# One stage of 160 units by token halves from the output projection to the store

## The chip, the cores and the metric

The kernel runs on one core of a Trainium2 chip. The time is that of the device in microseconds, the lower the better. The core's engines run their own queues and meet at semaphores: TensorE (PE) multiplies into PSUM, VectorE (DVE), ScalarE (ACT) and GpSimd (POOL) work on tiles in SBUF, VectorE and ScalarE also on PSUM, and SyncE (SP) issues the transfers.

## The reference

One residual block on 1024 tokens of width 1024. The part that matters begins when the two mixers, an RWKV-7 group and a sparse attention group, have written their rows:

```python
        mix = jnp.concatenate([y_rwkv, y_dsa], axis=-1).astype(x.dtype) @ w_out[i]
        x = x + rms_norm(mix, norm_mix_post[i])
        h = rms_norm(x, norm_ffn_pre[i])
        f = jnp.square(jax.nn.relu(h @ w_ffn1[i])) @ w_ffn2[i]
        x = x + rms_norm(f, norm_ffn_post[i])
        gate = jax.nn.sigmoid(rms_norm(x, norm_ple_pre[i]) @ w_ple_gate[i])
        x = x + rms_norm((p[i] @ w_ple[i]) * gate, norm_ple_post[i])
```

`rms_norm` divides each token by the root of the mean of its squares over the 1024 features and multiplies by a gain. The feed-forward width is 4096, p has 256 features.

## The kernel before

Everything lies feature-major: a tile is 128 features by tokens, eight such blocks are a full activation. Each fp32 operand of a large product is split into a rounded part (`hi`) and a remainder (`lo`), and a product is three matmuls, hi by hi, hi by lo and lo by hi. A weight tile is 128 x 1024 (512 KB): ScalarE rounds it (`Weights.round`, line 436), GpSimd subtracts (`Weights.remainder`, line 440), SyncE loads the next one into one of two slots when the remainder is made (line 431).

The stages run one behind the other, each in a block of its own with a barrier at its end. `project_out` multiplies the rows by 8 tiles of `w_out`, for both halves of 512 tokens per tile, and has the squares of its result added on GpSimd (line 215). `norms` then does the norm of the result, adds it to x and does the norm that the next product needs. For a half it takes the squares on ScalarE (line 203), sums them over the partitions with small matmuls on TensorE (lines 221 and 228), takes the root on ScalarE (line 234), inverts it and builds a diagonal on VectorE (lines 238 and 241), spreads it by a matmul (line 246), scales by it on VectorE (line 253), adds to x on VectorE and GpSimd in turn (lines 348 and 383), rounds on ScalarE (line 324) and takes the remainder on VectorE and GpSimd in turn (lines 353 and 390). `ffn` is a loop of 8 chunks of 4 up units (1024 features in, 128 out) and 4 down units (512 in, 256 out), each for all 1024 tokens, 48 matmuls. VectorE takes relu, square, rounding and remainder of an up unit (lines 573 to 577) and adds a down unit to the total (line 581). A second `norms` follows, then `per_layer`, 8 units of gate product, sigmoid on ScalarE (line 700), product with p (lines 737 to 739) and their product on VectorE (line 752), then `norms` once more and `store_x`, one transfer of 4 MB (line 1997).

The order on every engine is the order in which the code is written. The stages before the output projection are not touched.

## Time and profile before

| | us |
|---|---|
| median of 3 runs | 2121.1 (2120.21 to 2123.97) |
| the profiled execution | 2117.07 |
| its span, first to last instruction | 2115.2 |
| mean granted TensorE clock | 0.916 |
| output projection, first to last product | 1015.0 to 1110.5 |
| norms | 1110.5 to 1180.5 |
| feed-forward | 1180.5 to 1878.5 |
| norms | 1878.5 to 1959.0 |
| gate stage | 1959.0 to 2070.8 |
| last norm and store | 2070.8 to 2115.2 |

Positions are microseconds from the span's start. Busy time is that of instructions; waiting, branching and issuing transfers are not counted. Matmuls are pipelined: one is shown as some 390 ns long, though the next one starts sooner, so the distance of their starts is what a product costs. A granted clock of 1.0 is 2.4 GHz, 0.5 is 1.2 GHz. "out<-in" names the tile that is written and the tiles that are read, without their numbers.

### The profile page before, as it was taken

How to read it: one execution, taken by the hardware profiler on the slowest of the kernel's cores; microseconds unless marked ns; L12 is line 12 of the kernel's file. 1: busy time of each engine (PE TensorE's matmuls, PEld its weight loads, DVE VectorE, ACT ScalarE, POOL GpSimd, SP SyncE). 2: the span in 40 equal slices, each digit the busy share in tenths (PEclk: the TensorE clock that was granted, in tenths of full speed). 3: DMA queues.
4: the chain of work that ended last, by engine and by line, in shares of the span. 5: the costliest groups of instructions: out<-in, count | busy, mean ns of one | idle time of the engine just before them, and what ended most of it. 6: DMA issues, size and time to landing. Idle time of an engine off the chain costs nothing. (4 is left out here: it accounts for less than half of the span.)

```text
span 2115.2 us, 34729 instructions
## 1 busy us (share of the span) xinstructions
PE 1773.1 (84%) x14248; PEld 1438.6 (68%) x14248; DVE 1058.1 (50%) x1931; ACT 607.4 (29%) x963; POOL 516.3 (24%) x375
## 2 busy tenths in 40 slices
PE   1998976799399778886796799999999999966993
PEld 0776753488277667775576588888888888855782
...
GB/s 101 57 97 177 151 131 33 82 83 80 51 31 31 46 164 44 84 15 18 217 20 20 40 50 50 50 47 43 50 50 50 50 50 48 41 20 0 90 11 80
DMA packets 75002, 134.80 MB, mean 64 GB/s; under 512 B 5824, under 2 KB 49888, under 8 KB 74368
## 3 DMA queue, kind: packets, MB, share of 16 engines
...
## 5 line engine op out<-in xcount | busy, mean ns | idle before, releaser
L440 POOL TENSOR_TENSOR w_ffn_lo<-w_ffn_raw,w_ffn_hi 128x1024 fp32r<-128x1024 f32 x64 | 153.8, 2403 | 546.7 <-ACT w_ffn_hi L436 531.9
L436 ACT ACTIVATE w_ffn_hi<-w_ffn_raw 128x1024 fp32r<-128x1024 f32 x62 | 65.8, 1062 | 613.8 <-PE ffn_acc L463 319.2
L461 PE MATMUL ffn_acc<-h_hi,w_ffn_hi 128*128 128x512 f32 x512 | 200.0, 391 | 10.6 <-DVEq L565 10.6
L463 PE MATMUL ffn_acc<-h_hi,w_ffn_lo 128*128 128x512 f32 x512 | 199.7, 390 | 0.0
L462 PE MATMUL ffn_acc<-h_lo,w_ffn_hi 128*128 128x512 f32 x512 | 199.6, 390 | 0.0
L448 PE MATMUL ffn_acc<-ffn_hi,w_ffn_hi 128*128 128x512 f32 x512 | 199.2, 389 | 0.0
L449 PE MATMUL ffn_acc<-ffn_lo,w_ffn_hi 128*128 128x512 f32 x512 | 199.2, 389 | 0.0
L450 PE MATMUL ffn_acc<-ffn_hi,w_ffn_lo 128*128 128x512 f32 x512 | 199.2, 389 | 0.0
L581 DVE TENSOR_TENSOR y<-y,ffn_acc 128x2048 f32<-128x2048 f32 x32 | 73.2, 2288 | 240.5 <-PE ffn_acc L450 240.5
L461 PE MATMUL z_acc<-h_hi,w_in_first_hi 128*128 128x512 f32 x304 | 122.8, 404 | 15.1 <-ACTq L502 10.4
L573 DVE TENSOR_SCALAR ffn_relu<-ffn_acc 128x1024 f32<-128x1024 f32 x32 | 39.2, 1225 | 168.3 <-PE ffn_acc L463 168.3
L462 PE MATMUL z_acc<-h_lo,w_in_first_hi 128*128 128x512 f32 x304 | 120.4, 396 | 0.0
L463 PE MATMUL z_acc<-h_hi,w_in_first_lo 128*128 128x512 f32 x304 | 120.1, 395 | 0.0
L461 PEld LDWEIGHTS ffn_acc<-h_hi,w_ffn_hi 128*128 128x128 f32 x512 | 96.5, 188 | 32.2 <-DVEq L565 12.2
L462 PEld LDWEIGHTS ffn_acc<-h_lo,w_ffn_hi 128*128 128x128 f32 x512 | 96.5, 189 | 20.0
L463 PEld LDWEIGHTS ffn_acc<-h_hi,w_ffn_lo 128*128 128x128 f32 x512 | 96.4, 188 | 20.2
L448 PEld LDWEIGHTS ffn_acc<-ffn_hi,w_ffn_hi 128*128 128x128 f32 x512 | 96.1, 188 | 20.0
L450 PEld LDWEIGHTS ffn_acc<-ffn_hi,w_ffn_lo 128*128 128x128 f32 x512 | 96.1, 188 | 19.9
L449 PEld LDWEIGHTS ffn_acc<-ffn_lo,w_ffn_hi 128*128 128x128 f32 x512 | 96.1, 188 | 19.9
L575 DVE TENSOR_TENSOR ffn_square<-ffn_relu 128x1024 f32<-128x1024 f32 x32 | 106.1, 3315 | 1.1
L1731 DVE TENSOR_SCALAR_CACHE_REDUCE compared<-score,threshold 128x384 bf16<-128x384 f32 (+3 forms) x128 | 96.4, 810 | 1.1
L440 POOL TENSOR_TENSOR w_in_first_lo<-w_in_first_raw,w_in_first_hi 128x1024 fp32r<-128x1024 f32 x19 | 50.5, 2661 | 190.0 <-ACT w_in_first_hi L436 165.9
...
## 6 DMA issues: line engine op xcount, KB each, us to landing
w_ffn_raw<-w_ffn SPq DMA_DIRECT2D x64, 512.0 KB, 3.5
rwkv_factors<-factors_then_masks ACTq DMA_DIRECT2D x28, 512.0 KB, 6.3
...
w_in_first_raw<-w_in SPq DMA_DIRECT2D x19, 512.0 KB, 3.9
w_in_raw<-w_in SPq DMA_DIRECT2D x12, 512.0 KB, 3.9
x_in<-xT SPq DMA_DIRECT2D x8, 512.0 KB, 6.6
zT<-z_out SPq DMA_DIRECT2D x8, 512.0 KB, 2.9
w_out_raw<-w_out SPq DMA_DIRECT2D x8, 512.0 KB, 3.6
```

The lines of the kernel that those rows point to most:

```text
L436: act.activation(self.hi[u][:, :], self.raw[:, u, :], ACT.Copy).then_inc(self.rounded, 1)
L440: pool.tensor_tensor(self.lo[u][:, :], self.raw[:, u, :], self.hi[u][:, :].bitcast(F32), ALU.subtract).then_inc(self.split, 1)
L448: pe.matmul(acc[:, cut], w.hi[u][:, col], hi[:, k, cut], start=(k == 0), stop=False)
L449: pe.matmul(acc[:, cut], w.hi[u][:, col], lo[:, k, cut], start=False, stop=False)
L450: last = pe.matmul(acc[:, cut], w.lo[u][:, col], hi[:, k, cut], start=False, stop=(k == kblocks - 1))
L461: pe.matmul(acc[:, cut], w.hi[u][:, col], hi[:, k, cut], start=(k == 0), stop=False)
L462: pe.matmul(acc[:, cut], w.hi[u][:, col], lo[:, k, cut], start=False, stop=False)
L463: last = pe.matmul(acc[:, cut], w.lo[u][:, col], hi[:, k, cut], start=False, stop=(k == kblocks - 1))
L573: dve.tensor_scalar(relu[:, :], acc[:, u, 0, :], 0.0, None, ALU.max).then_inc(read, 1)
L575: link(dve.tensor_tensor(sq[:, :], relu[:, :], relu[:, :], ALU.mult))
L581: dve.tensor_tensor(total[:, m:m + 2, :], total[:, m:m + 2, :], acc[:, u, :, :], ALU.add).then_inc(read, 1)
L1731: last = dve.tensor_scalar(junk[t][:, :], score[t][:, :], thr[:, j:j + 1], None, ALU.is_ge, ALU.add, accum_out=count[:, j:j + 1])
```

## The change

`project_out`, `ffn`, `per_layer`, `store_x` and the three later uses of `norms` give way to one function, `from_mix_on`, with a single block. (`norms` keeps the input's norm alone, as `norm_of_input`, with the same instructions.) It runs 160 units in straight-line code, each for 512 tokens: 8 of the output projection for each half, 64 of the feed-forward for each half, 8 of the gate for each half. A unit is 24 matmuls, a gate unit has 6 more for p. The weight tiles are the same; each is loaded, rounded and split once per half, so 160 times instead of 80, in a ring of four slots. A slot is loaded when the unit that used it is multiplied, since `w_raw` and `w_lo` share their place. The remainder of the weights moves from GpSimd to VectorE. ScalarE takes relu and rounding of an up unit, VectorE the square and the remainder. A step s of an engine other than TensorE follows unit s - 1. The two tables `POST` and `PRE` say at which place each half's norm is summed and spread on TensorE, at which step it is inverted, and how many of its 8 blocks are done in each step from the first on: `Plan(sum, spread, invert, first, counts)`. x is loaded in two halves behind the rows, and the result is stored in eight transfers of 512 KB.

Cut to its core:

```diff
+    def add(self, pool, i, k):
+        if k > 0:
+            n = i * (KB - 1) + k - 1
+            pool.wait_ge(self.squared, i * KB + k + 1)
+            need(pool, self.added, n)
+            pool.tensor_tensor(self.total[:, :], self.total[:, :], self.sq[:, n % self.ring, :], ALU.add).then_inc(self.added, 1)
+    def sum(self, pe, i):
+        pe.wait_ge(self.added, (i + 1) * (KB - 1))
+        need(pe, self.rooted, i)
+        for t in range(self.QS):
+            last = pe.matmul(self.ps_mean[:, t:t + 1], self.total[:, t * P:(t + 1) * P], self.mean[:, 0:1], start=(t == 0), stop=(t == self.QS - 1))
+        last.then_inc(self.summed, 1)
...
+OUT0, OUT1, FFN0, FFN1, GATE0, GATE1, UNITS = 0, 8, 16, 80, 144, 152, 160
+CB4 = 4
+    POST = [Plan(8.5, 9, 8, 9, (3, 3, 2)), Plan(17, 18, 17, 18, (1,) * 8),
+            Plan(82, 83, 82, 83, (1,) * 8), Plan(145, 145.5, 144, 144, (3, 2, 3)),
+            Plan(153, 153.5, 152, 153, (2, 2, 2, 2)), Plan(UNITS, UNITS, UNITS, UNITS, (8,))]
+    PRE = [Plan(12, 12.75, 12, 13, (3, 3, 2)), Plan(27, 28, 27, 28, (1,) * 8),
+           Plan(92, 93, 92, 93, (1,) * 8), Plan(147.375, 148, 147, 148, (3, 3, 2))]
...
+    with Scope(nc) as same_place:
+        w_raw = same_place.sb("w_raw", [P, RING, KB * P], F32)
+        rows = same_place.sb("rows_raw", [P, KB, HALF], F32)
+        sq = same_place.sb("relu_squared", [P, 2, HALF], F32)
+    with Scope(nc) as ctx:
+        wl = ctx.sb("w_lo", [P, RING, KB * P], F32R)
...
+            for g in range(UNITS):
+                need(sp, multiplied, g - RING + 1)
+                sp.dma_start(w_raw[:, g % RING, :], weights(g)).then_inc(loaded[g % RING], 16)
+                if g == 0:
+                    load_rows(0)
+                if g == RING:
+                    load_rows(1)
+                    for h in range(NH):
+                        sp.dma_start(x[:, :, cut[h]], io["xT"][:, :, cut[h]]).then_inc(x_loaded[h], 16)
...
+            for k in range(0, KB, 2):
+                for v in range(2):
+                    wait_x(sp, 4, k + v)
+                sp.dma_start(io["out"][:, k:k + 2, cut[0]], x[:, k:k + 2, cut[0]]).then_inc(stored, 16)
...
+            for s in range(1, UNITS + 1):
+                g = s - 1
+                if is_up(g):
+                    n = up_before(g)
+                    act.wait_ge(multiplied, g + 1)
+                    need(act, up_ready, n - 1)
+                    act.activation(sq[:, n % 2, :], acc[:, 2 * (g % 2), :], ACT.Relu).then_inc(relued, 1)
+                i, blocks = mixed(s)
+                for k in blocks:
+                    act.wait_ge(freed, s)
+                    ny.square(act, i, k, y[:, k, cut[i % 2]])
+                if s == GATE0:
+                    act.wait_ge(multiplied, GATE0)
+                    act.wait_ge(ple_loaded, 16 * PB)
+                    act.activation(fh, ple_raw, ACT.Copy).then_inc(ple_rounded, 1)
+                    round_p(0)
+                if s == GATE1:
+                    act.wait_ge(multiplied, GATE1)
+                    round_p(1)
+                round_weights(s + 2)
+                if is_up(g):
+                    n = up_before(g)
+                    act.wait_ge(freed, s)
+                    act.activation(fh[:, n % CB4, :], sq[:, n % 2, :], ACT.Copy).then_inc(up_hi, 1)
+                if s <= KB:
+                    round_row(1, s - 1)
+                if GATE0 <= s < UNITS:
+                    j, h = (s - GATE0) % KB, half_of(s)
+                    act.wait_ge(gate_multiplied, s - GATE0 + 1)
+                    for k in (KB - 2, KB - 1):
+                        wait_x(act, 2 + h, k)
+                    act.wait_ge(ple_split, 2 + h)
+                    act.activation(y[:, j, cut[h]], acc[:, 2 * (s % 2), :], ACT.Sigmoid).then_inc(gated, 1)
+                for i, plan in enumerate(POST):
+                    if s == plan.invert:
+                        ny.take_root(act, i)
+                    if i < len(PRE):
+                        for k in plan.blocks(s):
+                            wait_x(act, i, k)
+                            nx.square(act, i, k, x[:, k, cut[i % 2]])
+                for i, plan in enumerate(PRE):
+                    if s == plan.invert:
+                        nx.take_root(act, i)
+                    for k in plan.blocks(s):
+                        act.wait_ge(nx.scaled, i * KB + k + 1)
+                        act.activation(hi[:, k, cut[i % 2]], normed[:, k % 2, :], ACT.Copy).then_inc(h_hi, 1)
+        @block.gpsimd
+        def _(pool):
+            for s in range(1, UNITS + 1):
+                i, blocks = mixed(s)
+                for k in blocks:
+                    ny.add(pool, i, k)
+                for i, plan in enumerate(POST):
+                    h = i % 2
+                    for k in plan.blocks(s):
+                        if k % 2:
+                            pool.wait_ge(ny.scaled, i * KB + k + 1)
+                            pool.wait_ge(x_loaded[h], 16)
+                            pool.tensor_tensor(x[:, k, cut[h]], x[:, k, cut[h]], y[:, k, cut[h]], ALU.add).then_inc(x_added[1], 1)
+                    if i < len(PRE):
+                        for k in plan.blocks(s):
+                            nx.add(pool, i, k)
+                for i, plan in enumerate(PRE):
+                    for k in plan.blocks(s):
+                        if k % 2:
+                            pool.wait_ge(h_hi, i * KB + k + 1)
+                            pool.tensor_tensor(lo[:, k, cut[i % 2]], normed[:, k % 2, :], hi[:, k, cut[i % 2]].bitcast(F32), ALU.subtract).then_inc(h_lo[1], 1)
...
+            def dense_unit(g):
+                h, b, out = half_of(g), g % RING, acc[:, 2 * (g % 2), :]
+                pe.wait_ge(split, g + 1)
+                need(pe, freed, g - 1)
+                for k in range(KB):
+                    norm_steps(g + k / KB)
+                    if g == OUT0:
+                        pe.wait_ge(rows_split, k + 1)
+                    if g == OUT1 and k == 0:
+                        pe.wait_ge(rows_split, 2 * KB)
+                    if g in (FFN0, FFN1, GATE0, GATE1):
+                        wait_lo(pe, (FFN0, FFN1, GATE0, GATE1).index(g) * KB + k)
+                    col = slice(k * P, (k + 1) * P)
+                    last = three(out, wh[:, b, col], wl[:, b, col], hi[:, k, cut[h]], lo[:, k, cut[h]], k == 0, k == KB - 1)
+                return last
+            def down_unit(g):
+                b = g % RING
+                norm_steps(g)
+                pe.wait_ge(split, g + 1)
+                need(pe, freed, g - 1)
+                done = up_before(g)
+                for k in range(CB4):
+                    if g % (2 * CB4) == CB4:
+                        pe.wait_ge(up_ready, done - CB4 + k + 1)
+                    for m in range(2):
+                        col = slice((2 * k + m) * P, (2 * k + m + 1) * P)
+                        last = three(acc[:, 2 * (g % 2) + m, :], wh[:, b, col], wl[:, b, col], fh[:, k, :], fl[:, k, :], k == 0, k == CB4 - 1)
+                last.then_inc(multiplied, 1)
...
+            for first in (GATE0, GATE1):
+                for g in range(first, first + KB):
+                    dense_unit(g).then_inc(gate_multiplied, 1)
+                    if g == first + 1:
+                        p_unit(first)
+                    if g > first:
+                        p_unit(g)
+            norm_steps(UNITS)
...
+            def read(g):
+                h, out = half_of(g), acc[:, 2 * (g % 2), :]
+                dve.wait_ge(multiplied, g + 1)
+                if g < FFN0:
+                    dve.tensor_copy(y[:, g % KB, cut[h]], out).then_inc(freed, 1)
+                elif is_up(g):
+                    n = up_before(g)
+                    dve.wait_ge(relued, n + 1)
+                    dve.scalar_tensor_tensor(sq[:, n % 2, :], out, 0.0, sq[:, n % 2, :], ALU.max, ALU.mult).then_inc(freed, 1)
+                elif is_down(g):
+                    m = 2 * (g % CB4)
+                    to, both = y[:, m:m + 2, cut[h]], acc[:, 2 * (g % 2):2 * (g % 2) + 2, :]
+                    if (g - FFN0) % (FFN1 - FFN0) < 2 * CB4:
+                        for k in (m, m + 1):
+                            wait_x(dve, h, k)
+                        dve.tensor_copy(to, both).then_inc(freed, 1)
+                    else:
+                        dve.wait_ge(freed, g - 2 * CB4 + 1)
+                        dve.tensor_tensor(to, to, both, ALU.add).then_inc(freed, 1)
+                else:
+                    to = y[:, (g - GATE0) % KB, cut[h]]
+                    dve.wait_ge(gated, g - GATE0 + 1)
+                    dve.tensor_tensor(to, to, acc[:, 2 * (g % 2) + 1, :], ALU.mult).then_inc(freed, 1)
+            for s in range(1, UNITS + 1):
+                g = s - 1
+                read(g)
+                split_weights(s + 1)
+                if is_up(g):
+                    n = up_before(g)
+                    dve.wait_ge(up_hi, n + 1)
+                    dve.tensor_tensor(fl[:, n % CB4, :], sq[:, n % 2, :], fh[:, n % CB4, :].bitcast(F32), ALU.subtract).then_inc(up_ready, 1)
+                if s == GATE0:
+                    dve.wait_ge(ple_rounded, 1)
+                    dve.tensor_tensor(fl, ple_raw, fh.bitcast(F32), ALU.subtract).then_inc(ple_split, 1)
+                    split_p(0)
+                if s == GATE1:
+                    split_p(1)
+                if s <= KB:
+                    split_row(1, s - 1)
+                for i, plan in enumerate(POST):
+                    h = i % 2
+                    if s == plan.invert:
+                        ny.invert(dve, i)
+                    for k in plan.blocks(s):
+                        block_y = y[:, k, cut[h]]
+                        ny.scale(dve, i, k, block_y, block_y, gains[:, POST_GAIN[i // 2], k:k + 1])
+                        if k % 2 == 0:
+                            dve.wait_ge(ny.scaled, i * KB + k + 1)
+                            dve.wait_ge(x_loaded[h], 16)
+                            dve.tensor_tensor(x[:, k, cut[h]], x[:, k, cut[h]], block_y, ALU.add).then_inc(x_added[0], 1)
...
-                    project_out(nc, io, rows + [y_attn[p] for p in range(PAIRS)], hi, lo, y, x, mix)
-                    norms(nc, common, x, y, pre=gains[:, FFN_PRE, :], hi=hi, lo=lo, w=w, tiles=io["w_ffn"], summed_y=mix)
-                ffn(nc, io, hi, lo, y, w)
...
-                norms(nc, common, x, y, gains[:, FFN_POST, :], gains[:, PLE_PRE, :], hi, lo, w=w, tiles=io["w_gate"])
...
-                per_layer(nc, io, hi, lo, y, w, gated)
-                norms(nc, common, x, y, summed_y=gated)
-            store_x(nc, x, io["out"])
+        from_mix_on(nc, io, rows + [y_attn[p] for p in range(PAIRS)], common, gains)
```

How the change moves instructions, at three places. TensorE, from the end of the output projection to the feed-forward, before: `mix_means` and `pre_means` are the sums, `mix_spread` and `pre_spread` the spreads.

```order
L450 MATMUL out_acc<-h_hi,w_out_lo 128x512
L221 MATMUL mix_means<-mean_column,mix_squares_total 128x1 x8
L590 UNCONDITIONAL_BRANCH
L326 UNCONDITIONAL_BRANCH
L246 MATMUL mix_spread<-mix_diagonal,ones 128x512 x2
L228 MATMUL pre_means<-mean_column,pre_squares 128x1 x36
L246 MATMUL pre_spread<-pre_diagonal,ones 128x512
L228 MATMUL pre_means<-mean_column,pre_squares 128x1 x28
L246 MATMUL pre_spread<-pre_diagonal,ones 128x512
L264 UNCONDITIONAL_BRANCH
```

TensorE in unit 8, the first of the second half, and at the start of unit 9, now.

```order
L783 MATMUL acc<-h_hi,w_lo 128x512
L510 MATMUL post_means<-mean_column,post_squares_total 128x1 x4
L781 MATMUL acc<-h_hi,w_hi 128x512
L782 MATMUL acc<-h_lo,w_hi 128x512
L783 MATMUL acc<-h_hi,w_lo 128x512
L781 MATMUL acc<-h_hi,w_hi 128x512
L782 MATMUL acc<-h_lo,w_hi 128x512
L783 MATMUL acc<-h_hi,w_lo 128x512
L781 MATMUL acc<-h_hi,w_hi 128x512
L782 MATMUL acc<-h_lo,w_hi 128x512
L783 MATMUL acc<-h_hi,w_lo 128x512
L781 MATMUL acc<-h_hi,w_hi 128x512
```

The sums and spreads of one half stand between the products of the other; before they stood together behind a barrier.

VectorE in the feed-forward, one up unit of the loop, before.

```order
L573 TENSOR_SCALAR ffn_relu<-ffn_acc 128x1024
L575 TENSOR_TENSOR ffn_square<-ffn_relu 128x1024
L115 REGISTER_ALU
L576 CAST ffn_hi<-ffn_square 128x1024
L115 REGISTER_ALU
L577 TENSOR_TENSOR ffn_lo<-ffn_square,ffn_hi 128x1024
```

VectorE in steps 17, 18 and the start of 19, now.

```order
L863 SCALAR_TENSOR_TENSOR relu_squared<-acc,relu_squared 128x512
L845 TENSOR_TENSOR w_lo<-w_raw,w_hi 128x1024
L891 TENSOR_TENSOR ffn_hi_lo<-relu_squared,ffn_hi_lo 128x512
L521 RECIPROCAL post_inverse<-post_root 128x4
L525 TENSOR_SCALAR post_diagonal<-norm_identity,post_inverse 128x128 x4
L863 SCALAR_TENSOR_TENSOR relu_squared<-acc,relu_squared 128x512
L845 TENSOR_TENSOR w_lo<-w_raw,w_hi 128x1024
L891 TENSOR_TENSOR ffn_hi_lo<-relu_squared,ffn_hi_lo 128x512
L536 SCALAR_TENSOR_TENSOR y<-y,gain_cols,post_spread 128x512
L910 TENSOR_TENSOR x<-x,y 128x512
L863 SCALAR_TENSOR_TENSOR relu_squared<-acc,relu_squared 128x512
```

The weights' remainder (`w_lo`) stands between the square and the activations' remainder, and norm work stands behind them.

ScalarE at the start of the gate stage, before (line 695 rounds the rows of p and `w_ple`).

```order
L695 ACTIVATE rows_hi<-y 128x1024 x4
L700 ACT_TABLE_LOAD
L700 ACTIVATE gate<-gate_acc 128x1024
L436 ACTIVATE w_gate_hi_20<-w_gate_raw 128x1024
L700 ACTIVATE gate<-gate_acc 128x1024
```

ScalarE in step 144 and into step 145, now (line 733 is the sigmoid, line 516 the root).

```order
L715 ACTIVATE ffn_hi_lo<-y 128x2048
L693 ACTIVATE p_hi_lo<-y 128x1024
L685 ACTIVATE w_hi<-w_raw 128x1024
L733 ACT_TABLE_LOAD
L733 ACTIVATE y<-acc 128x512
L516 ACT_TABLE_LOAD
L516 ACTIVATE post_root<-post_means,eps 128x4
L497 ACTIVATE pre_squares_total<-x 128x512
L497 ACTIVATE pre_squares<-x 128x512 x2
L497 ACTIVATE post_squares_total<-y 128x512
L685 ACTIVATE w_hi<-w_raw 128x1024
```

Roots and sigmoids alternate there, each with a table load, where one table load stood before the first sigmoid.

## Rows read from the trace of the kernel before

**Rows 1.** Windows: stretch, its us, busy us of PE, PEld, DVE, ACT, POOL, clock, DMA share, GB/s.
```profile
1015.00:1110.50 95.50, 92.82 (x384) 73.46 (x384) 18.97 (x15) 19.87 (x26) 32.98 (x19) 0.97 0.28 103
1110.50:1180.50 70.00, 37.76 (x152) 32.28 (x152) 40.52 (x69) 23.32 (x40) 33.22 (x20) 0.53 0.05 15
1180.50:1878.50 698.00, 697.94 (x3072) 577.55 (x3072) 284.53 (x160) 65.82 (x62) 148.62 (x62) 1.00 0.15 47
1878.50:1959.00 80.50, 38.51 (x153) 33.48 (x153) 51.20 (x83) 30.70 (x54) 30.66 (x18) 0.53 0.04 14
1959.00:2070.80 111.80, 111.08 (x480) 90.94 (x480) 13.18 (x11) 26.34 (x33) 28.30 (x17) 0.99 0.13 47
2070.80:2115.20 44.40, 7.42 (x20) 4.18 (x20) 19.55 (x35) 2.85 (x5) 17.11 (x12) 0.54 0.22 95
1023.00:1035.00 12.00, 9.38 (x39) 6.67 (x38) 4.90 (x4) 2.68 (x3) 0.00 (x0) 1.00 1.02 420
```

**Rows 2.** The timeline of TensorE, output projection: start us, duration us, instruction; first and last of 151.
```profile
1040.28 0.40 PE L448 MATMUL out_acc<-h_hi,w_out_hi 128*128 128x512 f32 x1
...
1075.28 0.40 PE L448 MATMUL out_acc<-h_hi,w_out_hi 128*128 128x512 f32 x1
```

**Rows 3.** Groups from 1000 us on: busy us, mean ns of one, idle before.
```profile
L436 ACT ACTIVATE w_ffn_hi<-w_ffn_raw 128x1024 fp32r<-128x1024 f32 x62 | 65.8, 1062 | 613.8 <-PE ffn_acc L463 319.2 <-PE ffn_acc L450 294.5
L203 ACT ACTIVATE pre_squares<-x 128x512 f32<-128x512 f32 x32 | 19.6, 628 | 41.4 <-PE pre_means L228 33.6 <-DVE x L348 5.8 <-POOL x L383 2.0
L575 DVE TENSOR_TENSOR ffn_square<-ffn_relu 128x1024 f32<-128x1024 f32 x32 | 106.1, 3315 | 1.1
L581 DVE TENSOR_TENSOR y<-y,ffn_acc 128x2048 f32<-128x2048 f32 x32 | 73.2, 2288 | 240.5 <-PE ffn_acc L450 240.5
L577 DVE TENSOR_TENSOR ffn_lo<-ffn_square,ffn_hi 128x1024 fp32r<-128x1024 f32 x32 | 39.2, 1225 | 1.1
L253 DVE SCALAR_TENSOR_TENSOR normed_x<-x,gain_cols,pre_spread 128x512 f32<-128x512 f32 x32 | 22.6, 741 | 11.1 <-PE pre_spread L246 8.8 <-POOL h_lo L390 2.3
L440 POOL TENSOR_TENSOR w_ffn_lo<-w_ffn_raw,w_ffn_hi 128x1024 fp32r<-128x1024 f32 x64 | 153.8, 2403 | 546.7 <-ACT w_ffn_hi L436 531.9 <-ACT w_ffn_hi L416 14.8
L383 POOL TENSOR_TENSOR x<-x,normed_y 128x512 f32<-128x512 f32 x24 | 39.6, 1650 | 73.9 <-DVE normed_y L253 73.9
L215 POOL TENSOR_TENSOR mix_squares_total<-mix_squares_total,mix_squares 128x512 f32<-128x512 f32 x14 | 18.0, 1289 | 13.6 <-ACT mix_squares L203 12.2 <-POOL mix_squares_total L215 0.4
```

**Rows 4.** The timelines of SyncE and ScalarE: first load and first copy of the output projection.
```profile
1003.46 0.82 SPq L431 DMA_DIRECT2D w_out_raw<-w_out  x2
1010.40 1.06 ACT L619 ACTIVATE h_hi<-rows_raw 128x1024 fp32r<-128x1024 f32 x1 [17.79 <-DMA rows_raw<-y_rwkv]
```

**Rows 5.** The timeline of TensorE: a norm's sum at full clock, its two spreads at half.
```profile
1113.75 1.05 PE L221 MATMUL mix_means<-mean_column,mix_squares_total 128*128 128x1 f32 x8 [3.32 <-POOL mix_squares_total L215]
...
1118.57 2.08 PE L246 MATMUL mix_spread<-mix_diagonal,ones 128*128 128x512 f32 x2 [1.74 <-DVE mix_diagonal L241]
```

**Rows 6.** The DMA view: count, KB each, median us from issue to landing.
```profile
w_ffn_raw<-w_ffn SPq DMA_DIRECT2D x64, 512.0 KB, 3.5
x<-xT SPq DMA_DIRECT2D x1, 4096.0 KB, 15.6
out<-x SPq DMA_DIRECT2D x1, 4096.0 KB, 11.1
```

**Rows 7.** The timelines of ScalarE, VectorE and SyncE in the tail.
```profile
2077.70 1.28 ACT L234 ACT_TABLE_LOAD   x1 [4.43 <-PEq L672]
2079.00 0.42 ACT L234 ACTIVATE gated_root<-gated_means,eps 128x4 f32<-128x4 f32 x2
2082.55 1.41 DVE L253 SCALAR_TENSOR_TENSOR normed_y<-y,gain_cols,gated_spread 128x512 f32<-128x512 f32 x2 [2.17 <-PE gated_spread L246]
2084.47 1.40 DVE L253 SCALAR_TENSOR_TENSOR normed_y<-y,gain_cols,gated_spread 128x512 f32<-128x512 f32 x2
2103.66 0.34 SPq L1997 DMA_DIRECT2D out<-x  x1
```

592 lines of the change are left out of this document (255 added, 337 removed).

## The prediction

> **What bounds the kernel now.** I read the stage windows first [rows 1]. From the output projection on, TensorE has 3936 matmuls of 512 columns (384 + 3072 + 480), and it is the engine everybody waits for. In the feed-forward stage they fill the window: 698 us for 3072, less about 1.6 us in which the first ones ran at 1.2 GHz, is 0.2267 us each. So 3936 of them cost 892.3 us. The stretch from the first (1015.0) to the last (2070.8) takes 1055.8 us, an excess of 163.5 us. It lies in two windows in which the granted clock is 0.53 and hardly a product runs: 70.0 us of norms before the feed-forward and 80.5 us after it. The rest is 8.5 us in the output projection (95.5 less 87.0), 1.7 in the feed-forward and 3.0 in the gate stage (111.8 less 108.8). Behind the last product stand 44.4 us of last norm and store. The other 1015 us of the program are untouched.
>
> **Products.** Their number stays: 160 units of 24 and 16 units of 6. The spacing could change. The same three matmuls stood 0.2333 us apart in the output projection (150 of them between the two rows of [rows 2]: 35.00 us), where two halves of an accumulator alternate in straight-line code. The straight-line gate code ran at 108.8 + 3.0 us for 480, so straight lines alone don't cost that. I take 0.2267, the value of 3552 of the 3936; the other end is a rival.
>
> **What leaves.** The two norm windows go, 150.5 us, since their work is written between the units. The 8.5 + 1.7 + 3.0 us go as well and are built anew below.
>
> **TensorE's own norm work** now stands between products. Nine half norms lie before the last product. Each has a sum, 1.05 us at the full clock, and a spread matmul, 2.08 us at half clock [rows 5], so 1.04 at the full one: 2.1 x 9 = 18.9 us. The ends are 18.9 and 33 (all at half clock); the engine is busy on both sides, so I take the first.
>
> **The feeding of a unit.** A unit is 5.44 us. Per unit, ScalarE now rounds a weight tile (1.06), VectorE takes its remainder (1.22, as line 577; it was GpSimd's 2.40), and 128 tiles are loaded and split where 64 were. An up unit adds on ScalarE relu and copy (0.63 each, as a square) and on VectorE 0.74 and 0.68 us: 2.3 and 2.6 us of 5.44. A down unit adds 1.15 on VectorE (half of line 581) [rows 3]. Traffic doubles from 47 GB/s, far under the 420 GB/s of the window at 1023 [rows 1]. A load is issued when its slot's unit ends, lands 3.5 us later [rows 6] and is rounded in the step that begins 5.44 us after issue: 1.9 us spare, and one more unit behind that. The tightest spot is the first down unit of a chunk. The fourth block of activations is ready after relu 0.8, square 0.75, copy of weights and copy (VectorE's remainder runs beside them), remainder 0.68: 3.5 us; TensorE asks for it after 18 matmuls, 4.08 us. Cover: 0.6 us. So nothing, except in the five windows in which norm blocks delay ScalarE by about a microsecond and GpSimd holds VectorE: 0 to 8, I take 3 us. That holding is in [rows 3]: line 575, two operands in SBUF, takes 3.32 us beside a 2.40 us GpSimd instruction, line 577 without one 1.22; line 581, which reads PSUM, is not stretched.
>
> **New waits on TensorE, in order.**
> (a) Unit 5. Behind the end of unit 0 SyncE queues a weight tile, eight half rows, all of x and then tile 5: 7 MB. At 420 GB/s that is 17 us, at the rate of the row of x (4 MB in 15.6 us [rows 6]) 26 us. Unit 5 is due 21.8 us after unit 0 and needs 2.3 us of rounding and remainder: 0 to 6.6, I take 4.
> (b) Unit 8 needs the second half's last row, rounded only in the step after unit 7: VectorE's copy 0.7, ScalarE square 0.63, weights 1.06, row 0.63, VectorE 0.68, hand-overs 0.2: 3.9 us.
> (c) Unit 12 begins with the sum of the first pre-norm. Between the ends of unit 8 and unit 11, 18.4 us with the spread and sum, GpSimd must do 4 additions to x (1.65), 7 additions of squares and 2 of the other half (1.29): 18.2 us, from 4.2 us on. 22.4 without a clash, 25 with some: 4 to 7, I take 6.
> (d) Gate stage. After unit 143 ScalarE does 2 squares, a copy of 2048 columns (2.1), one of 1024, a weight tile, waits for VectorE's two remainders (8.1 us from the unit's end), then table load and sigmoid (1.28 + 0.6), table load and root (1.28 + 0.3), VectorE's diagonal 1.1: 12.7. TensorE asks at 5.44 + 1.05 + 2.72 = 9.2: 3.5 us. Unit 146's remainder comes 0.7 late. The sum at 147.375 waits for the same GpSimd chain, 3.9. The root at 148 stands behind the sigmoid of 147 and one table load: 0.6 + 1.28 + 0.3 + 1.1 + 0.3 = 3.6, of which the six p matmuls cover 1.4: 2.2. Sum 10.3, I take 10, ends 3 and 18.
> (e) Half clock: 2.5 us at the start, my share of the output projection's 8.5, and 1.6 after each of two longer waits, as at the start of the feed-forward: 5.5 (estimate; ends 2 and 12).
> Sum: 18.9 + 3 + 4 + 3.9 + 6 + 10 + 5.5 = 51.3 us of excess where there were 163.5.
>
> The trace shows a table load as 1.28 us with the root 0.02 us behind it [rows 7]. The Trainium skill ("ScalarE: Activation LUTs", What ACT_TABLE_LOAD costs) gives about 2.66 us for a switch, with a drain of 1.38 behind the load. Four switches stand on the path, so by that page the sum would be 5.5 us larger; by the row it stays.
>
> **Start.** ScalarE's first copy was at 1010.40, behind 1 MB of weights and a 512 KB row issued from 1003.46 on [rows 4]. Now 512 KB and 256 KB stand ahead: about 1.8 us at 420 GB/s. Then 0.63 + 1.06 + 1.22: 1011.8 for 1015.0 (GpSimd's slower remainder is gone). I take 1012.
>
> **Tail** [rows 7]. Before: 2070.8 to 2115.2. Now only half a norm: read 0.7, square 0.63, add 1.3, sum 1.2, table load and root 1.6, diagonal 1.1, spread 2.1, with hand-overs 9.3 us; then four pairs at 1.93 us (2084.47 less 2082.55 in the same chain), of which the last ends with GpSimd's 1.65: 8.9; then the last store is 512 KB, not 4 MB, so 3.5 us, as a weight load, in place of 11.1, and 0.9 around it. 22.6 us for 44.4.
>
> **Sum.** 1012 + 892.3 + 51.3 + 22.6 = 1978.2 us of span for 2115.2. The profiled execution took 1.9 us more than its span, and the median stands 4.0 over that execution: 1984 us, 6.5% less.
>
> **Rivals.**
> *Matmuls at 0.2333 us in all units*: 3936 x 0.0066 = 26 us more, 2010 us. For it: straight-line code with weights and operands at new places, and two accumulators alternating in down units. Against it: down units before alternated too, inside the 698 us. It decides at any mean spacing near 0.233. Chance 0.12.
> *The norms stay on the path*: TensorE passes each `norm_steps` in program order, and a late sum stops all products behind it. If the 150.5 us come back as waits of 8 to 18 us at the nine half norms, in place of the 27 us of waits that I count: 123 us more, 2107 us. For it: GpSimd's 18 us of work in 18 us at (c). Against it: elsewhere the table leaves 2 to 9 units between a block and the sum that needs it. Chance 0.06. That the edit does not do what it says is this case.
> *Weights come late (slower)*: one mechanism. A slot is refilled only after its unit is multiplied; the ring has four. Landing time L, about 3 us of rounding and remainder in their steps, and the unit itself make one turn of four units: (L + 3 + 5.44) / 4. It decides from L = 13.3 us on; the stage is as long as before at 0.86 us more per unit, L = 16.8. At L = 20 a unit is 7.1 us: about 2250 us. For it: 128 tiles are fetched for the same matmuls as 64 were, and by (a) tile 5 takes 17 us or more behind x. Against it: 3.5 us alone and traffic at a quarter of what was reached. Chance 0.05 for this or another loss.
> *No waits at all*: (a) to (d) and the five windows nil, 27 us less, 1957.
>
> **Numbers.** Forecast 0.77, with 1957 inside it. Range 1955 to 2028: from no waits to the spacing rival with 18 us more of waits; it leaves out 2107 and the slower case, and some of the forecast's own spread. A measurement here can tell 0.2%, about 4 us. Faster 0.94, same 0.01, slower 0.05.
>
> **What would show it.** Feed-forward units at 5.44 us with TensorE's busy share at 100% over units 16 to 143, 128 x 5.44 = 696 us; idle time of TensorE named by GpSimd's additions at unit 12, by VectorE's h_lo at unit 8, by the diagonal in the gate stage; weight landing of 3.5 us; last product near 1956, end 22.6 us later. Wrong if `w_lo` or `ffn_hi_lo` stands as releaser in every unit, if the spacing is 0.233, or if the waits at sums exceed 30 us.

## The result: 5.9% faster, with 64.2 us of excess where 51.3 was forecast

The changed kernel took 1993.3 us (median of four runs, 1991.4 to 2002.9) where the kernel before took 2120.7 on the same chip: ratio 0.941, 95% interval 0.938 to 0.944. The profiled execution has a span of 1991.1 us and took 1992.56. The forecast was 1984 us with a range of 1955 to 2028.

The windows of the changed kernel: units 0 to 15, units 16 to 143, the gate stage, and what follows the last product. Columns as in [rows 1]. (An fp32 matmul of a sum or a spread shows as two records, so the counts hold some more than the products.)

```profile
1012.10:1130.50 118.40, 101.50 (x405) 81.36 (x405) 61.98 (x80) 44.85 (x65) 41.25 (x28) 0.90 0.41 140
1130.50:1834.10 703.60, 703.60 (x3113) 581.93 (x3112) 341.76 (x388) 226.71 (x307) 58.56 (x44) 1.00 0.30 98
1834.10:1968.60 134.50, 120.22 (x510) 96.69 (x509) 68.98 (x85) 55.97 (x76) 50.28 (x34) 0.95 0.21 71
1968.60:1991.10 22.50, 3.51 (x12) 1.45 (x10) 11.38 (x18) 2.17 (x3) 6.31 (x5) 0.63 0.25 94
```

The two windows at a clock of 0.53 in [rows 1], 70.0 and 80.5 us, are gone. In the feed-forward window TensorE is busy all the time at the full clock: 3072 matmuls at 0.2267 us are 696.3 us, and four half norms on TensorE are the other 7.3. What is left to gain stands in the first and the third window: 118.4 us for 87.0 us of products, and 134.5 for 108.8. Excess is, as in the prediction, what the stretch from the first product to the last takes beyond 3936 products of 0.2267 us (892.3 us): 956.5 less 892.3 is 64.2 us.

The page's groups and DMA issues of the changed kernel (busy us, mean ns; KB each, us to landing), which answer to [rows 3, 6]:

```profile
L685 ACT ACTIVATE w_hi<-w_raw 128x1024 fp32r<-128x1024 f32 x160 | 168.4, 1052 | 155.2 <-DMA w_raw<-w_ffn 144.3
L845 DVE TENSOR_TENSOR w_lo<-w_raw,w_hi 128x1024 fp32r<-128x1024 f32 x160 | 203.3, 1271 | 1.3 <-ACT w_hi L685 1.3
L504 POOL TENSOR_TENSOR post_squares_total<-post_squares_total,post_squares 128x512 f32<-128x512 f32 x42 | 64.6, 1539 | 570.9 <-ACT post_squares L497 570.1
...
w_raw<-w_ffn SPq DMA_DIRECT2D x128, 512.0 KB, 3.4
```

A weight tile lands in 3.4 us though twice as many are fetched, and the remainder costs VectorE 1.27 us. GpSimd's additions of squares have a mean of 1.54 us where those of [rows 3] had 1.29: here something holds them (the run with the remainder on GpSimd shows what).

The waits of TensorE by what ended them (us in total, times, longest):

```profile
PE acc L781 <- DVE w_lo L845: 19.5, 5, 12.5
PE pre_means L510 <- POOL pre_squares_total L504: 14.4, 2, 8.1
PE post_spread L531 <- DVE post_diagonal L525: 3.9, 1, 3.9
PE acc L781 <- DVE h_lo L849: 3.7, 1, 3.7
PE pre_spread L531 <- DVE pre_diagonal L525: 2.2, 1, 2.2
```

The longest of the first line, 12.5 us, is the start of unit 0, before the first product. The others are 31.2 us. None lies in the feed-forward stage. Where they stand, on TensorE's timeline (start, duration, in brackets the idle time before):

```profile
1046.54 0.79 PE L781 MATMUL acc<-h_hi,w_hi 128*128 128x512 f32 x1 [4.58 <-DVE w_lo L845]
1047.13 0.63 PE L782 MATMUL acc<-h_lo,w_hi 128*128 128x512 f32 x1
1047.56 0.63 PE L783 MATMUL acc<-h_hi,w_lo 128*128 128x512 f32 x1
...
1069.80 0.75 PE L781 MATMUL acc<-h_hi,w_hi 128*128 128x512 f32 x1 [3.73 <-DVE h_lo L849]
...
1103.33 1.84 PE L510 MATMUL pre_means<-mean_column,pre_squares_total 128*128 128x1 f32 x8 [8.07 <-POOL pre_squares_total L504]
...
1847.32 1.38 PE L531 MATMUL post_spread<-post_diagonal,ones 128*128 128x512 f32 x2 [3.86 <-DVE post_diagonal L525]
```

They are units 5, 8 and 12 and the spread at 145.5, in the prediction's order (a) to (d). The starts behind the wait at 1046.54 are 0.43 us apart, and the granted clock from there to 1052.6 is 0.50: 1.2 GHz. The same follows the waits of 3.7, 8.1, 3.9 and 6.3 us. The waits of 1.3 and 2.2 us in the gate stage were not followed by it. So each of the longer waits is paid a second time, in part. In the whole stretch 51 matmuls stand at that distance, 10.2 us; four of them are the start of unit 0.

From here on kernels are compared by the stretch from the first of the 3936 products to the last, 956.5 us in the changed kernel, read from one profiled execution each. In these executions its start moved between 1012 and 1022 us though the code ahead is the same, which is noise of several us in the times. The stretch has noise too: the gate window, which the next three runs don't touch, took 133.7, 135.8 and 133.9 us in them for 134.5, so a price read from the stretch is good to one or two us.

### The profile page after: what moved, and what is told of

Same layout as the page of the kernel before. It is cut to its first block and busy times, and to the rows that moved or that the text cites. A ratio compares the mean times of both kernels' runs of the same rounds, so it can differ in the third digit from the quotient of the medians.

```text
span 1991.1 us, 34351 instructions
## 1 busy us (share of the span) xinstructions
PE 1716.8 (86%) x14024; PEld 1387.2 (70%) x14024; DVE 1114.5 (56%) x2131; ACT 765.3 (38%) x1192; POOL 379.1 (19%) x337
## 5 line engine op out<-in xcount | busy, mean ns | idle before, releaser
L781 PE MATMUL acc<-h_hi,w_hi 128*128 128x512 f32 x768 | 309.3, 403 | 23.2 <-DVE w_lo L845 19.5
L782 PE MATMUL acc<-h_lo,w_hi 128*128 128x512 f32 x768 | 303.8, 396 | 0.0
L783 PE MATMUL acc<-h_hi,w_lo 128*128 128x512 f32 x768 | 303.4, 395 | 0.0
L685 ACT ACTIVATE w_hi<-w_raw 128x1024 fp32r<-128x1024 f32 x160 | 168.4, 1052 | 155.2 <-DMA w_raw<-w_ffn 144.3
L845 DVE TENSOR_TENSOR w_lo<-w_raw,w_hi 128x1024 fp32r<-128x1024 f32 x160 | 203.3, 1271 | 1.3 <-ACT w_hi L685 1.3
L781 PE MATMUL acc<-ffn_hi_lo,w_hi 128*128 128x512 f32 x512 | 200.2, 391 | 0.0
L782 PE MATMUL acc<-ffn_hi_lo,w_hi 128*128 128x512 f32 x512 | 199.3, 389 | 0.0
L783 PE MATMUL acc<-ffn_hi_lo,w_lo 128*128 128x512 f32 x512 | 199.3, 389 | 0.0
L781 PEld LDWEIGHTS acc<-h_hi,w_hi 128*128 128x128 f32 x768 | 147.2, 192 | 58.4 <-DVE w_lo L845 21.9
L782 PEld LDWEIGHTS acc<-h_lo,w_hi 128*128 128x128 f32 x768 | 147.6, 192 | 32.2 <-issue 1.9
L401 PE MATMUL z_acc<-h_hi,w_in_first_hi 128*128 128x512 f32 x304 | 122.9, 404 | 14.4 <-ACTq L442 10.4
L782 PEld LDWEIGHTS acc<-ffn_hi_lo,w_hi 128*128 128x128 f32 x512 | 96.2, 188 | 20.3 <-issue 0.5
L781 PEld LDWEIGHTS acc<-ffn_hi_lo,w_hi 128*128 128x128 f32 x512 | 96.1, 188 | 20.3 <-issue 0.5
```

Of the source, the lines that this page charges most:

```text
L401: pe.matmul(acc[:, cut], w.hi[u][:, col], hi[:, k, cut], start=(k == 0), stop=False)
L685: act.activation(wh[:, g % RING, :], w_raw[:, g % RING, :], ACT.Copy).then_inc(rounded, 1)
L781: pe.matmul(out, w_hi, a_hi, start=first, stop=False)
L782: pe.matmul(out, w_hi, a_lo, start=False, stop=False)
L783: return pe.matmul(out, w_lo, a_hi, start=False, stop=last)
L845: dve.tensor_tensor(wl[:, b, :], w_raw[:, b, :], wh[:, b, :].bitcast(F32), ALU.subtract).then_inc(split, 1)
```

## Experiments

### x behind tiles 6 and 8

```diff
                 if g == RING:
                     load_rows(1)
-                    for h in range(NH):
-                        sp.dma_start(x[:, :, cut[h]], io["xT"][:, :, cut[h]]).then_inc(x_loaded[h], 16)
+                if g in (6, 8):
+                    h = (g - 6) // 2
+                    sp.dma_start(x[:, :, cut[h]], io["xT"][:, :, cut[h]]).then_inc(x_loaded[h], 16)
```

> The two halves of x are issued by SyncE behind the weight tiles of units 6 and 8 instead of ahead of the tile of unit 5. Theory (a): the wait of 4.7 us ahead of unit 5 is the weight tile standing behind 7 MB in the queue; with x later it is gone, and so is the stretch at half clock behind it (3 us): about 8 us less, 1985 us. Unit 8 (3.9 us) and unit 12 (8.2 us) wait as before, so the gain is not given back. Rival: the tile is late because of the eight half rows alone, or the matmuls behind only start the next wait earlier (GpSimd's work for unit 12 is then the limit, which starts from the end of unit 8): the wait at unit 5 stays above 3 us or unit 12's grows by as much, and the time stays near 1993.

Measured: 1987.9 us, the stretch 948.1, 8.4 less. Unit 5 has no wait any more, nor half clock behind it; units 8 and 12 wait 3.7 and 8.1 us as before. The window of units 0 to 15 is 110.7 us for 118.4, so 7.7 of the 8.4 lie where the change acts. The theory (about 8 us) holds, and the gain isn't given back.

### And the rows of the second half two per step

```diff
-                if s <= KB:
-                    round_row(1, s - 1)
+                if 3 <= s <= 6:
+                    round_row(1, 2 * s - 6)
+                    round_row(1, 2 * s - 5)
...
-                if s <= KB:
-                    split_row(1, s - 1)
+                if 3 <= s <= 6:
+                    split_row(1, 2 * s - 6)
+                    split_row(1, 2 * s - 5)
```

> As the kernel with x later, and in addition the eight rows of the second half are rounded and split two in each of the steps 3 to 6 instead of one in each of the steps 1 to 8. Theory (b): unit 8 waits 3.9 us because the last row is handled in the step after unit 7, behind VectorE's copy and ScalarE's square and weight tile; with all rows done two steps earlier the wait is gone, and with it the slow clock behind it: 4 to 6 us less than x later alone, 12 to 14 us less than the changed kernel, about 1980. Rival: two rows per step cost ScalarE 2.1 and VectorE 2.4 us more of a 5.44 us unit, or the rows have not landed by step 3 (they stand in the queue ahead), so that units 4 to 7 wait instead: 1984 or more.

Measured: 1984.1 us, the stretch 943.8, another 4.3 less. The row `h_lo L849` is gone from TensorE's waits, and units 4 to 7 don't wait. The window of units 0 to 15 gave 6.3 us (104.4 for 110.7), the upper end of the expectation; the stretch shows less because the gate window came out 2.1 longer. (b) holds.

### The first pre norm's sum 1.5 units later

```diff
-    PRE = [Plan(12, 12.75, 12, 13, (3, 3, 2)), Plan(27, 28, 27, 28, (1,) * 8),
+    PRE = [Plan(13.5, 14.25, 13, 14, (3, 3, 2)), Plan(27, 28, 27, 28, (1,) * 8),
```

> The first pre-norm's sum of squares moves on TensorE from the head of unit 12 to the middle of unit 13, with its root, spread and blocks by one unit or so. Theory (c): GpSimd needs about 26 us from the end of unit 8 for its additions, and the sum asks after 18; 8.2 us of wait, and half clock of some 3 us behind it, go: about 10 us less, 1983. The sum at unit 16's side must still be in time: 0 to 2 us of wait there. Rival: the sum is late for a reason that moves with it (GpSimd is held by VectorE's work in each unit), so that the wait is only shorter by the 8 us that the sum is moved if nothing else moves, and the first feed-forward unit waits instead for its blocks: 1988 to 1993.

Measured: 1988.5 us, the stretch 946.8, 9.7 less, although unit 5 happened to wait 1.1 us longer in this execution. What came back is small:

```profile
PE pre_means L510 <- POOL pre_squares_total L504: 6.7, 1, 6.7
...
PE acc L781 <- DVE h_lo L921: 1.2, 1, 1.2
PE acc L781 <- POOL h_lo L768: 0.3, 1, 0.3
```

One of the two waits at `pre_means` is left, that of the gate stage, and unit 16 waits 1.5 us for its last rows. The median alone, 1988.5, lies in the rival's band of 1988 to 1993 (its four executions took 1985.8 to 1996.9), so the windows decide: units 0 to 15 took 107.2 us for 118.4, and 2.1 us came back in the feed-forward window, at unit 16. GpSimd's own chain did not change: its last addition ahead of the sum ended 25.3 us after the end of unit 8, as before (25.2). (c) holds: GpSimd needs a fixed time, and the sum that asks 1.5 units later, 8.2 us, finds it done.

### The weights' remainder on GpSimd again

```diff
         @block.gpsimd
         def _(pool):
+            split_weights(0)
+            split_weights(1)
             for s in range(1, UNITS + 1):
+                split_weights(s + 1)
...
         @block.vector
...
                 read(g)
-                split_weights(s + 1)
```

> The weights' remainder is taken on GpSimd again, as in the kernel before the change, and not on VectorE; all else is the changed kernel. Theory: GpSimd is what is late at the sums of units 12 and 147.375 (8.2 and 6.5 us of wait). With 160 instructions of 2.4 us more it gets about 2.4 us per unit more to do, so over the three to four units between a post block and the sum some 7 to 10 us more of wait at each of the two sums, and the first unit starts about 1 us later: 15 to 25 us more, 2008 to 2018. The plain feed-forward units stay at 5.44 us. Rival: VectorE and GpSimd hold each other by turns whoever takes the remainder, and VectorE is the one relieved (203 us less busy): the waits stay within 3 us of what they are and the time stays near 1993.

Measured: 2018.9 us, the stretch 977.1, 20.6 more. The sum of the expectation is right and its places are wrong. Unit 12 waits only 1.2 us more, the sum at 147.375 2.2 us less. 14.4 us of the 20.6 are in the feed-forward window (718.0 for 703.6), whose plain units the expectation had left at 5.44 us, and 5.4 in units 0 to 15. TensorE's waits at unit 8 (3.7 before), at unit 5 (4.6 before) and at the first down unit of eleven chunks:

```profile
PE acc L790 <- DVE h_lo L852: 7.6, 1, 7.6
PE acc L790 <- DVE y L862: 6.5, 1, 6.5
PE acc L790 <- DVE ffn_hi_lo L890: 6.3, 11, 0.6
```

and the group behind the last of them:

```profile
L890 DVE TENSOR_TENSOR ffn_hi_lo<-relu_squared,ffn_hi_lo 128x512 fp32r<-128x512 f32 x64 | 138.4, 2163 | 44.9 <-ACT ffn_hi_lo L724 44.9
```

The remainder of an activation block takes VectorE 2.16 us here and 0.68 in the changed kernel, as the same instruction: it has two operands in SBUF and stands beside GpSimd's 2.4 us, which is the pattern of lines 575 and 577 in [rows 3]. So the gain of the move is in the main not time on GpSimd but that the short instructions behind which TensorE waits aren't held. The Trainium skill ("SBUF — State Buffer", SBUF: two separate sides) says that VectorE with two inputs in SBUF and GpSimd share one pair of ports, and that whichever starts first keeps the other out for its whole instruction; by that, and by the trace, GpSimd can be held too. That explains unit 12. GpSimd's timeline in the changed kernel:

```profile
1091.76 5.38 POOL L504 TENSOR_TENSOR pre_squares_total<-pre_squares_total,pre_squares 128x512 f32<-128x512 f32 x3
1097.10 2.24 POOL L504 TENSOR_TENSOR post_squares_total<-post_squares_total,post_squares 128x512 f32<-128x512 f32 x1
```

and VectorE's beside it:

```profile
1095.91 2.31 DVE L845 TENSOR_TENSOR w_lo<-w_raw,w_hi 128x1024 fp32r<-128x1024 f32 x1
```

From 1082.0 to 1103.2 GpSimd did the thirteen additions that stand ahead of the sum, in 21.2 us. At 1.28 us each, as they take alone, they would have been 16.6, so some 4 us are holding, as in the 2.24 us beside VectorE's 2.31 (1.22 alone). With the remainder on GpSimd the same stretch took 23.2 us, of which two remainders are 4.7. So the change took 4.7 us of work off GpSimd ahead of this sum and gave back 2.7 of them in holding; it is elsewhere that it pays. The rows above also show that the two hold each other in turn: GpSimd's third addition ends at 1097.14, VectorE's remainder 1.1 us later, at 1098.22, and GpSimd's next addition 1.1 us after that, at 1099.34. Each takes about its time alone once the other has ended, which agrees with that rule.

### The gate stage's two norms later

```diff
-            Plan(82, 83, 82, 83, (1,) * 8), Plan(145, 145.5, 144, 144, (3, 2, 3)),
+            Plan(82, 83, 82, 83, (1,) * 8), Plan(145, 146.125, 144, 145, (3, 2, 3)),
...
-           Plan(92, 93, 92, 93, (1,) * 8), Plan(147.375, 148, 147, 148, (3, 3, 2))]
+           Plan(92, 93, 92, 93, (1,) * 8), Plan(149.5, 150.5, 149, 150, (4, 4))]
```

> The two half norms of the gate stage are moved in the plan alone: the post norm's spread from 145.5 to 146.125 with its blocks a step later, the pre norm's sum from 147.375 to 149.5, its spread from 148 to 150.5, its blocks to steps 150 and 151. Theory (d): the waits of 4.0 us (spread), 6.5 us (sum) and 2.4 us (spread) and the stretches at half clock behind them go; with unit 146's remainder 18 us at most, I expect 14 to 18 us less, 1976 to 1979. Some wait may come back at unit 152, whose rows are then handled in the two steps ahead of it: 0 to 2 us. Rival: the root stands behind a sigmoid whatever its step is and the diagonal holds VectorE ahead of the read of the accumulator, so that the waits turn into waits of the next unit: under 6 us less, 1987 or more.

Measured: 1981.8 us, the stretch 942.9, 13.6 less. The gate stage's window is 120.3 us for 134.5, so it gave 14.2, the low end of the expectation, at a clock of 1.00 for 0.95:

```profile
1835.00:1955.30 120.30, 116.05 (x510) 93.17 (x510) 70.47 (x85) 55.95 (x76) 51.63 (x34) 1.00 0.24 79
```

(d) holds. Nothing is left at the spread and 0.5 us at the sum, and units 152 and 153 take some 3 us that they had not, of which 2.0 are waits (0.2, 1.4 and 0.4).

### All four together

> All moves together: x later, the second half's rows two per step, the first pre norm's sum at 13.5 (its blocks four each in steps 14 and 15, so that unit 16 does not wait), and the gate stage's two norms later. If the waits are independent, their prices add: 8.4 + 4.3 for the first two as measured, 9.7 for the first sum with up to 1.4 more at unit 16, 14 to 18 in the gate stage: 36 to 40 us less than the changed kernel, about 1955. From the first product to the last start the changed kernel has 956.5 us; this one would have 918, of which 892.3 are products and 17 norm work. Rival: GpSimd or VectorE is the true limit in the first 16 units and the waits come back as one of 5 to 10 us at unit 16: 1962 or more.

Measured in five runs: 1960.1 us (1956.4 to 1965.5), ratio to the kernel before 0.923 (0.920 to 0.926), the stretch 919.6, 36.9 less. The four prices (8.4, 4.3, 9.7, 13.6) make 36.0, so they add, at the low end of the expected 36 to 40; the median is 5 us over the 1955 that was expected. Windows as above:

```profile
1012.10:1105.60 93.50, 93.16 (x404) 75.89 (x405) 60.90 (x77) 41.91 (x61) 40.70 (x26) 0.98 0.51 176
1105.60:1810.50 704.90, 703.88 (x3113) 581.68 (x3112) 344.41 (x392) 228.02 (x309) 60.18 (x45) 1.00 0.31 98
1810.50:1931.70 121.20, 117.35 (x510) 94.31 (x509) 70.47 (x85) 55.96 (x76) 51.62 (x34) 0.99 0.24 79
```

27.3 us of excess are left, of which 16.4 are the nine half norms' own matmuls. It is the fastest kernel of this study.

### Loads one unit later

```diff
-                need(sp, multiplied, g - RING + 1)
+                need(sp, multiplied, g - RING + 2)
```

> Each weight tile's load is issued one unit (5.44 us) later than the ring of four would allow, so that it lands 3.4 us after the step that rounds it has begun, as if a load took 8.9 us from issue to landing. By the turn of the ring alone (threshold 13.3 us) nothing is late: 1993. By the chain at the head of a chunk's first down unit (0.6 us of cover on the prediction's count) ScalarE stands in its wait for the tile, and its copy of the relu behind it: ready 3.5 + 1.06 + 0.6 + 0.7 = 5.9 us after the unit's end where TensorE asks at 4.1, 1.7 us at each of the 16 chunks, 27 us more, 2020; a little more at the norm units.

Measured: 2043.9 us, the stretch 1004.8, 48.3 more, where 27 and a little more was expected. The tiles still land 3.4 us after they are issued; with the 5.44 us that they are held back this stands for 8.9. The ring's turn alone is refuted: 8.9 us is far below its threshold of 13.3, and costs 2.4%. The chain at the head of a chunk shows as it was told, in every chunk:

```profile
PE acc L781 <- DVE ffn_hi_lo L891: 27.2, 16, 2.7
```

and one of the sixteen on the timeline of the three engines:

```profile
1303.51 1.06 ACT L685 ACTIVATE w_hi<-w_raw 128x1024 fp32r<-128x1024 f32 x1 [2.79 <-DMA w_raw<-w_ffn]
1304.47 0.61 ACT L724 ACTIVATE ffn_hi_lo<-relu_squared 128x512 fp32r<-128x512 f32 x1
1305.11 0.69 DVE L891 TENSOR_TENSOR ffn_hi_lo<-relu_squared,ffn_hi_lo 128x512 fp32r<-128x512 f32 x1 [2.47 <-ACT ffn_hi_lo L724]
1305.86 0.50 PE L781 MATMUL acc<-ffn_hi_lo,w_hi 128*128 128x512 f32 x1 [1.70 <-DVE ffn_hi_lo L891]
```

ScalarE waits for the tile with the copy of the activations queued behind it, and TensorE for that: 16 waits, 27.2 us. By windows, the feed-forward stage is 40.2 us longer (743.8 for 703.6), 2.5 us for each of its 16 chunks, of which 1.7 is the wait; the rest stands around the waits, in part as half clock (76 matmuls at 0.43 us in the whole stretch for 51, 5 us). Units 0 to 15 are 6.0 us longer and the gate stage 2.1, where the same tile is late elsewhere.

### Where the tiles lie

The spacing rival had asked whether new places of the operands could cost 0.0066 us per matmul. In the changed kernel they don't: 0.2267 in every stage (within 0.001), the output projection too, which had 0.2333 before. What makes 0.2333? First the order of the matmuls, in the kernel before:

```diff
-                for k in range(KB):
-                    if j == 0:
+                if j == 0:
+                    for k in range(KB):
                         pe.wait_ge(split, k + 1)
-                    last = dense_block(pe, acc[:, u, :], w, u, hi, lo, k, KB, P, 0)
+                        last = dense_block(pe, acc[:, u, :], w, u, hi, lo, k, KB, P, 0)
+                else:
+                    last = dense(pe, acc[:, u, :], w, u, hi, lo, KB, P, 0)
```

> The kernel before, where in the output projection a unit's two halves of an accumulator no longer alternate from row to row: one half's 24 matmuls stand ahead of the other's (the first unit excepted, whose rows come one by one). In the changed kernel the output projection has 0.2267 us per matmul, in the kernel before 0.2333. If the alternation makes the difference, 336 of its 384 matmuls go to 0.2267: 2.2 us less there, which the times can hardly tell (0.1%) and the records can. Rival: the difference comes from elsewhere (where the weights or rows lie, or traffic beside them), and the spacing stays at 0.2333.

Measured: 2124.1 us, ratio 1.001 (0.999 to 1.003), and 0.2333 us in the units with one half ahead of the other. The alternation isn't the cause. Then the place of the weights, once in the changed kernel and once in the one before:

```diff
+        ctx.sb("gap", [P, 16], F32)
         wh = ctx.sb("w_hi", [P, RING, KB * P], F32R)
```

> The changed kernel with 64 unused bytes per partition ahead of the tile w_hi, which so lies 64 bytes further in SBUF; nothing else differs. In the kernel before, the tiles of w_out stand 64 bytes off the multiple of 128 at which those of w_ffn and w_gate stand, and only their matmuls took 0.2333 us. If the place of the weights sets the spacing, matmuls from w_hi (2624 of the 3936) go to about 0.233 and those from w_lo stay at 0.2267, or all three do if the spacing is set by pairs: 17 to 26 us more, 2010 to 2019. Rival: the place has no part in it, 1993.

Measured: 2012.3 us, ratio 0.949 (0.945 to 0.952) where the changed kernel has 0.941; the stretch 971.6, 15.0 more. A feed-forward window without a wait or norm work shows it, as the count of matmuls (PE, x) in 35 us at a clock of 1.00:

```profile
1300.00:1335.00 35.00, 35.00 (x153) 28.44 (x152) 15.30 (x17) 9.38 (x12) 0.00 (x0) 1.00 0.33 103
```

Down units' three matmuls stand 0.226, 0.236 and 0.232 us apart, mean 0.231. The third of them has weights from w_lo and activations that have not moved, and is slower all the same, so the spacing does not hang on an instruction's own operands alone.

> The kernel before with 64 unused bytes per partition ahead of the tiles of w_out, which brings them to the same place modulo 128 bytes as those of w_ffn. If the place sets the spacing, the output projection's matmuls go from 0.2333 to 0.2267 us, 2.5 us less. Rival: it stays at 0.2333, and what is left is where the accumulator lies in PSUM or which tensors are beside it.

Measured in one run (2137.7 us, with the first product only at 1034.0): 0.2324 us for 0.2333, in a new pattern of 0.228 to 0.241; the forecast of 0.2267 is wrong. So the place plays a part here too, but the place modulo 128 bytes alone does not set the spacing. Two more kernels, with one run each. 128 bytes ahead of w_hi:

```diff
+        ctx.sb("gap", [P, 32], F32)
         wh = ctx.sb("w_hi", [P, RING, KB * P], F32R)
```

> The changed kernel with 128 unused bytes per partition ahead of w_hi instead of 64. If the spacing hangs on where w_hi lies modulo 128 bytes relative to the rows, it is back at 0.2267 us and the time at that of the changed kernel, 1993. If every distance from the original place costs, the three matmuls stay near 0.226, 0.236 and 0.232, about 2012.

And 64 bytes ahead of all tiles:

```diff
+        same_place.sb("gap_a", [P, 16], F32)
         w_raw = same_place.sb("w_raw", [P, RING, KB * P], F32)
...
+        ctx.sb("gap_b", [P, 16], F32)
         wl = ctx.sb("w_lo", [P, RING, KB * P], F32R)
```

> The changed kernel with 64 unused bytes per partition ahead of all its tiles, so that w_hi, w_lo and the rows h_hi and h_lo lie 64 bytes further together. If the spacing hangs on the distance between weights and rows, it stays at 0.2267 us, 1993; if on the place of the weights itself, it is 0.231 or more in all three, 2010 to 2020.

Measured: with 128 bytes 2025.1 us and 0.2333 us in the mean (0.233, 0.232 and 0.235 in the three matmuls), the stretch 23.1 us longer; with all tiles moved together 0.2267 us and a stretch of 956.5, to the tenth that of the changed kernel (its 2001.5 us come from a start at 1021.0). The same window with 128 bytes:

```profile
1300.00:1335.00 35.00, 35.00 (x152) 28.17 (x151) 14.27 (x14) 8.68 (x11) 0.00 (x0) 1.00 0.28 90
```

and with all tiles moved:

```profile
1300.00:1335.00 35.00, 35.00 (x156) 28.97 (x155) 14.28 (x14) 8.71 (x12) 0.00 (x0) 1.00 0.27 90
```

(A count takes in the matmuls that the window cuts; the spacings are read from neighbours.) In the last kernel w_hi lies at the very place where, moved alone, it cost 15.0 us. So what counts is the distance between w_hi and the tiles ahead of it, not where it lies: undisturbed 0.2267, 64 bytes off 0.231, 128 bytes off 0.233. To which of those tiles (w_lo, the activations, or the tiles that no matmul reads) the distance counts, the runs don't separate. For the kernel before this is a likeness and no proof: by the sizes of the tiles between them (8192, 32, 32, 4096 and 4096 bytes) and of w_ffn's own (24,576), w_out began 41,024 bytes behind w_ffn, 64 more than a multiple of 8 KB; but its price was that of 128 bytes here (0.2333), and 64 bytes more made it 0.2324. At what distances the price is nil beyond that was not run, and why it is paid stays open.

## Why the prediction was right, and where its terms were off

- **What bounds the kernel, and what leaves.** Right. TensorE's products bound it; the two norm windows went (150.5 us), and nothing came in their place in the feed-forward stage, since sums stand units behind their squares there.
- **Products.** Right: 0.2267 us in all 3936. The row of [rows 2] belonged to the place of that stage's tiles. The rival had chance 0.12 on "weights and operands at new places", and that is a real mechanism: 64 bytes ahead of w_hi cost 15.0 us of the 26 that it named, 128 bytes 23.1.
- **TensorE's norm work.** Four half norms cost the feed-forward window 7.3 us: 1.8 each (0.9 for a sum and 0.9 for a spread) for 2.1, and so 16.4 us in all for 18.9.
- **The feeding of a unit.** Right in kind: no waits where 3 us were taken. The 0.6 us of cover at a chunk's first down unit was right enough to foretell 16 waits of 1.7 us when loads come 5.44 us later. VectorE's remainder was taken at 1.22 and has a mean of 1.27.
- **(a)** 4.6 us for 4; of its ends the upper is low, since 7 MB at the rate of the row of x take 27 us and not 26. **(b)** 3.7 for 3.9. **(c)** 8.1 for 6. The sum could start 25.3 us after the end of unit 8, the prediction's upper count; the step that failed is when TensorE asks, 18.4 us after it. It was 17.2, since the sum of the other norm lies inside unit 8. And 6 was taken where 25 less 18.4 gives 6.6.
- **(d)** 3.9, 1.3, 6.3 and 2.2 us for 3.5, 0.7, 3.9 and 2.2: 13.7 for 10. The step that failed is "the same GpSimd chain, 3.9": it was counted without a clash, and its twelve additions took 2.8 us more than 1.28 us each, these two rows 2.2 of them:

```profile
1859.55 3.54 POOL L504 TENSOR_TENSOR pre_squares_total<-pre_squares_total,pre_squares 128x512 f32<-128x512 f32 x2 [0.74 <-ACT pre_squares L497]
...
1867.22 5.07 POOL L504 TENSOR_TENSOR pre_squares_total<-pre_squares_total,pre_squares 128x512 f32<-128x512 f32 x3
```

- **(e) Half clock.** The largest error, and the term that was mis-sized. 5.5 us were taken, for the start and two long waits; 51 matmuls at 1.2 GHz cost 10.2 us, behind the start and five waits, and longer sums, spreads and first matmuls around the waits most of the 7.5 us that are left of the excess. The waits at units 5, 8 and 12 (4.6, 3.7 and 8.1 us) brought 3.2, 1.8 and 4.0 us of excess beside themselves.
- **Start.** 1012.1 for 1012. That was luck in part: other executions began up to 10 us later, and the prediction's own terms (1010.4, 1.8 less, then 0.63, 1.06 and 1.22) add up to 1011.5 where it wrote 1011.8.
- **Tail.** 22.5 for 22.6, from errors that cancel. The chain to the first scaled block took 7.8 us for 9.3, and what follows the last pair 3.5 for 4.4; the four pairs with GpSimd's last addition took 11.1 for 8.9, 2.55 us a pair for 1.93, since line 910, with two operands in SBUF, takes 1.20 us beside GpSimd and 0.69 alone:

```profile
1976.40 0.75 DVE L536 SCALAR_TENSOR_TENSOR y<-y,gain_cols,post_spread 128x512 f32<-128x512 f32 x1 [2.15 <-PE post_spread L531]
1977.19 0.69 DVE L910 TENSOR_TENSOR x<-x,y 128x512 f32<-128x512 f32 x1
...
1979.23 1.20 DVE L910 TENSOR_TENSOR x<-x,y 128x512 f32<-128x512 f32 x1
```

- **Sum.** 1012.1 + 892.3 + 64.2 + 22.5 is 1991.1, the measured span. The span came out 12.9 us above the forecast's, and all of it is the excess, 12.9 above its term. Around the span stood 1.5 us for 1.9, and the median 0.7 us over the profiled execution for 4.0, which took back 3.7 of the error.
- **Table loads.** The changed kernel's loads take 1.28 us too and what follows starts at once (one runs from 1856.54 to 1857.82, and its sigmoid starts at 1857.84), so the sum by the row stood, and the larger figure of the Trainium skill ("ScalarE: Activation LUTs", What ACT_TABLE_LOAD costs) isn't seen here. (d) was off, but by GpSimd, not by this.
- **The slower rival.** It did not come about (3.4 us to landing), but its threshold was wrong. With loads held back so that they land as after 8.9 us the stretch was already 48 us longer: the ring's turn isn't what is tight, ScalarE's order is, in which a wait for a weight tile stands ahead of the copy that TensorE needs.
